# The first branch's triangular inverses on four 64x64 quarters of TensorE

## The chip, the cores and the metric

The kernel runs on one core of one Trainium2 chip. The metric is the device time of one execution in microseconds; the time before is the median of three runs. One more execution was profiled, and all rows of the trace below are from it. The engines are named as in the profile: PE is TensorE (matmuls), PEld its weight loads, DVE is VectorE, ACT is ScalarE, POOL is GpSimd.

## What is computed

The program is a small hybrid network on 256 tokens of 2048 channels: two attention layers (stages "L"), then one layer with two recurrent branches beside each other. The change touches only the first branch, a delta-rule recurrence with 16 heads of 64 channels that runs over 512 tokens (256 of the context, then 256 of the input) in both directions:

```python
def rwkv7_scan(r, decay, k, v, kk, b, s0, reverse, with_out):
    ...
    def step(s, inp):
        dec_t, k_t, v_t, kk_t, b_t = inp[:5]
        sa = jnp.einsum('bhvk,bhk->bhv', s, kk_t)
        s = (s * dec_t[:, :, None, :] - sa[..., None] * b_t[:, :, None, :]
             + v_t[..., None] * k_t[:, :, None, :])
```

The second branch is `gdn_chunked`, the gated delta rule with 8 heads of 128 channels, on the same tokens in both directions. Both are evaluated by chunks of 128 tokens. In a chunk the steps are coupled by a triangular matrix with ones on its diagonal, whose inverse is needed for each head, chunk and direction.

## The kernel before

**Stages.** The stages follow each other: L (two attention layers), P (projections of the recurrent layer), B (the two branches), C and M (merge and MLP). Stage B lies between about 1940 and 2875 us of the span.

**Threads of stage B.** A written order runs in stage B. Each engine has one instruction stream, and `Weave.run` makes it by taking one step (up to the next `yield`) of each stream in turn: `thread_a(0)`, `thread_b(0)`, `thread_a(1)`, `thread_b(1)`, then the tails and the bases. `thread_a(d)` is the first branch in direction d, for eight pairs of heads c = 0..7: `prep`, `scores`, `inverse`, `chain`. `thread_b(d)` is the second branch, for eight heads. So a step of an inverse of the first branch stands between steps of the other threads, on every engine, and engines take their streams in order. Direction 1 of a pair begins when direction 0 is 8 steps into its inverse (the word `middle`), so the two inverses of a pair don't overlap each other; the inverse of one direction lies beside the chain or the preparation of the other.

**An inverse.** For one (c, d) of the first branch there are eight 128x128 triangular matrices (2 heads x 4 chunks), in `NA`, 512 columns for a head. The inverse is built by doubling: `X` holds the inverses of the diagonal blocks of width w = 1, 2, 4, ... 32, and `XP` their transposes, for both 64-blocks of a matrix, which stand on the two halves of the partitions (0 to 63 and 64 to 127) with 64 columns for each matrix. Levels lv = 1 to 5 each do: `iq`, the product of NA's diagonal 64-blocks with X (16 matmuls of 64x64x64); DVE copies with a mask what lies beside the blocks into `Q` (L2555); `ix` and `it`, XP with Q and Q with XP (16 matmuls each); ACT copies the new halves of the blocks into X (its copies all stand at L1325), DVE those of XP (L2562), and POOL puts the identity back into Q (L3150). Level 0 is a masked copy (L2541, L2550). Level 6 joins the two 64-blocks: 8 matmuls from one partition half into the other, twice.

**Quarters of the array.** A 64x64x64 matmul takes its operands from one half of the partitions and writes one half of the partitions of a bank of PSUM, and so stands in one of four 64x64 quarters of the array: (rows, columns) = (low, low), (high, high), (low, high), (high, low). In levels 0 to 5 an operand's half is also its result's half, so only the first two quarters are used. The matmuls of level 6 all stand in a single crossed quarter. The second branch's inverse does the same with four matrices (`n == 4`), and it isn't changed. An fp32 matmul of the program is two MATMUL instructions in the profile, and each has its LDWEIGHTS.

**Banks.** Each direction of the first branch has a ring of two PSUM banks (`DR[d]`: banks 0 and 1, banks 2 and 3). The function `bank()` waits until the copy out of the bank's last use is done. `iq`, `ix` and `it` take a bank each, in turn.

## Time and profile before

| | us |
|---|---|
| median of 3 runs | 3850.47 |
| lowest, highest | 3849.56, 3851.57 |
| profiled execution, its own time | 3848.72 |
| its span on the core | 3846.6 |

The span is what the rows count in; 2.1 us of the execution lie around it, and the profiled execution is 1.75 us below the median of the three.

### The profile page before, as it was taken

Reading aid. Unit: us, or ns where it says so; the run is one execution under the profiler, and the core shown is the slowest. Engines: PE = TensorE matmul, PEld = TensorE weight load, DVE = VectorE, ACT = ScalarE, POOL = GpSimd, SP = SyncE. Lnnn points to the kernel's source line nnn. Section 1 sums busy time; section 2 is a strip of 40 time slices with the busy share of each in tenths; the row PEclk is TensorE's granted clock in tenths of the full one; section 3 lists DMA queues with packets and bytes.
Section 4 is the critical chain, followed back from the end, with each engine's and each line's share of the span. In section 5 each row is a group of like instructions: output and inputs, shape, how many; then the busy total and the mean of one; then the engine's idle time right before and its main releaser. Section 6 shows DMA issues by size and latency. Waiting matters only on the chain. (4 is left out here: it accounts for less than half of the span.)

```text
span 3846.6 us, 85962 instructions
## 1 busy us (share of the span) xinstructions
PE 3682.1 (96%) x37216; PEld 3409.0 (89%) x37216; DVE 2084.0 (54%) x3808; ACT 1504.8 (39%) x2641; POOL 1659.3 (43%) x1195
## 2 busy tenths in 40 slices
PE   7999999999998999999899999999988999999998
PEld 7999898999986888888688888888888999999998
DVE  5545425444336776677766666666547553435343
ACT  5344434444434432322233333333334453435353
POOL 5555556555544543333311111111115566666664
PEclk9999999999989999999999999999999999999999
DMA  6445454454445777778410000100007445455553
GB/s 238 169 180 181 187 196 156 167 185 176 175 154 175 259 261 266 250 258 293 154 32 20 15 24 28 28 20 15 3 2 263 176 176 187 177 186 184 179 186 131
DMA packets 116391, 587.20 MB, mean 153 GB/s; under 512 B 20912, under 2 KB 40496, under 8 KB 51376
## 3 DMA queue, kind: packets, MB, share of 16 engines
q1 hardware_dynamic: 116016, 581.71, 42.5%
q8 instruction: 295, 4.83, 0.5%
q14 instruction: 80, 0.66, 0.1%
HBM read 560.95 MB, written 20.71 MB: 151 GB/s over the span
## 5 line engine op out<-in xcount | busy, mean ns | idle before, releaser
L557 PE MATMUL bank<-act_L,part_L 128*128 128x256 f32 x7296 | 946.6, 288 | 12.4 <-DMA cst<-in_cst 4.6
L557 PEld LDWEIGHTS bank<-act_L,part_L 128*128 128x128 f32 x7296 | 901.0, 193 | 49.1 <-issue 30.6
L557 PE MATMUL bank<-act_P,part_P 128*128 128x512 f32 (+1 forms) x3488 | 716.1, 365 | 17.9 <-POOL part_P L3013 12.8
L3013 POOL TENSOR_TENSOR part_L<-wring,part_L 128x512 fp32r<-128x512 f32 x304 | 532.8, 1754 | 458.0 <-ACT part_L L1325 449.7
L3013 POOL TENSOR_TENSOR part_C<-wring,part_C 128x512 fp32r<-128x512 f32 x320 | 567.6, 1782 | 370.1 <-ACT part_C L1325 370.1
L557 PEld LDWEIGHTS bank<-act_P,part_P 128*128 128x128 f32 x3488 | 590.4, 188 | 136.9 <-DVE arena_P L2437 16.0
L557 PE MATMUL bank<-arena_B 64*64 64x64 f32 (+2 forms) x11200 | 544.4, 231 | 39.2 <-DVE arena_B L2550 21.0
L557 PEld LDWEIGHTS bank<-arena_B 64*64 64x64 f32 (+2 forms) x11200 | 481.3, 143 | 89.2 <-DVE arena_B L2550 23.4
L3013 POOL TENSOR_TENSOR part_P<-wring,part_P 128x512 fp32r<-128x512 f32 x184 | 306.1, 1669 | 428.1 <-ACT part_P L1325 428.1
L1325 ACT ACTIVATE part_C<-wring 128x1024 fp32r<-128x1024 f32 x320 | 338.4, 1058 | 355.8 <-PE bank L557 352.7
L557 PE MATMUL bank<-act_Y,part_C 128*128 128x258 f32 (+1 forms) x3840 | 463.7, 283 | 9.5 <-POOL part_C L3013 9.5
L557 PEld LDWEIGHTS bank<-act_Y,part_C 128*128 128x128 f32 x3840 | 462.9, 190 | 9.7 <-issue 9.7
L2040 DVE TENSOR_TENSOR part_L<-wring,part_L 128x512 fp32r<-128x512 f32 x304 | 239.5, 789 | 426.0 <-ACT part_L L1325 425.8
L557 PE MATMUL bank<-act_C,part_C 128*128 128x256 f32 x3840 | 468.5, 283 | 0.0
L557 PEld LDWEIGHTS bank<-act_C,part_C 128*128 128x128 f32 x3840 | 462.6, 192 | 0.0
L1325 ACT ACTIVATE part_L<-wring 128x1024 fp32r<-128x1024 f32 x304 | 320.6, 1056 | 293.5 <-PE bank L557 293.5
L2040 DVE TENSOR_TENSOR part_C<-wring,part_C 128x512 fp32r<-128x512 f32 x320 | 235.7, 736 | 297.9 <-ACT part_C L1325 297.8
L2101 DVE SCALAR_TENSOR_TENSOR arena_P<-arena_P,mods 128x512 f32<-128x512 f32 x240 | 272.8, 1137 | 8.1 <-DMA arena_P<-in_w 4.6
L2040 DVE TENSOR_TENSOR part_P<-wring,part_P 128x512 fp32r<-128x512 f32 x184 | 170.2, 925 | 190.9 <-ACT part_P L1325 190.8
L1325 ACT ACTIVATE part_P<-wring 128x1024 fp32r<-128x1024 f32 x184 | 191.2, 1053 | 153.0 <-PE bank L557 152.4
L3150 POOL COPY arena_B<-cst 128x256 f32<-128x256 f32 x80 | 32.5, 407 | 455.2 <-PE bank L557 455.2
L1325 ACT ACTIVATE arena_B<-bank 128x128 f32<-128x128 f32 (+4 forms) x296 | 111.2, 394 | 216.9 <-PE bank L557 119.3
(250 smaller groups left out, 3483.0 us busy)
## 6 DMA issues: line engine op xcount, KB each, us to landing
wring<-in_w SPq DMA_DIRECT2D x404, 1024.0 KB, 4.8
arena_P<-in_w SPq DMA_DIRECT2D x64, 1024.0 KB, 5.2
mring<-in_w SPq DMA_DIRECT2D x32, 1024.0 KB, 6.6
z_kept<-arena_P SPq DMA_DIRECT2D x34, 256.0 KB, 5.6
z_kept<-arena_P SPq DMA_DIRECT2D x58, 128.0 KB, 5.4
xT<-z_kept SPq DMA_DIRECT2D x26, 256.0 KB, 2.8
arena_C<-z_kept SPq DMA_DIRECT2D x32, 128.0 KB, 3.4
cst<-z_kept SPq DMA_DIRECT2D x24, 128.0 KB, 2.1
```

Source lines behind the costliest of these rows:

```text
L557: return e.matmul(out, lhsT, rhs, start=start, stop=stop)
L1325: return e.activation(out, a, ACT.Copy, scale=scale)
L2040: tt(wl[:, 0:4, :], wring[s % NS][:, 8 * j:8 * j + 4, :], wh[:, 0:4, :].bitcast(F32), sub).then_inc(*mark("dve_lo", "lov", stage, h))
L2101: z = ts(a, x, c, None, mult, None) if row == 0 else stt(a, x, c, a, mult, add)
L3013: e.tensor_tensor(wl[:, 4:8, :], wring[s % NS][:, 8 * j + 4:8 * j + 8, :], wh[:, 4:8, :].bitcast(F32), sub).then_inc(*mark("pool_lo", "lop ...
L3150: e.tensor_copy(region(Q[lv % 2], wd, d), same).then_inc(*mark(sem, "qf", tag, lv))
```

## The change

The first branch's inverses get functions of their own, `inverse_a`. Level 1 to 5 are computed with half of the eight matrices "straight" (as before) and half "crossed": of these, the block that stands on the low half is written to the high half and the other one to the low half. Which four of them cross changes with the level (`STRAIGHT`, `CROSSED`, `staying`, `moving`: pairs of matrices), so that operands always meet on one half. The matmuls are written in the order straight low, straight high, crossed low, crossed high, again and again. The straight ones write one bank of the ring, the crossed ones the other, so each of the two steps of a level takes both banks. Since a crossed result moves the whole transposed block, XP is copied whole for the four that move. The copies are now divided by bank: of `iq` two masked copies on DVE; of `it` two copies on ACT (from the straight bank) and two on DVE (from the crossed bank). `ix` and `it` are one step with one semaphore increment at its end. The transposes of level 0 are set by four masked copies instead of two. The masks (`lev2`) are twice as wide. Levels 0 and 6 have the matmuls that they had, and the number of steps (`yield`) of an inverse is the same. The threads, the loads and the other stages aren't touched.

```diff
@@ -545,6 +545,19 @@
 
         LATE_A, LATE_B, LATE_TA, LATE_TB, FIRST_B = 2, 3, 0, 0, 4
         CTXAT = (6, 8, 10, 12)
+
+
+        STRAIGHT = (slice(0, 4, 3), slice(0, 4, 2))
+        CROSSED = (slice(1, 3), slice(1, 4, 2))
+
+        def staying(lv):
+            return slice(0, 2) if lv < 5 else slice(0, 4, 2)
+
+        def moving(lv):
+            return slice(2, 4) if lv < 5 else slice(1, 4, 2)
+
+        def units(pairs):
+            return [2 * s + i for s in range(4)[pairs] for i in range(2)]
         GLA_LEAD, GLA_MORE = 3, 2
 
 
@@ -1026,6 +1039,80 @@
+            def inverse_a(tag, ring, NA, X, XP, Q):
...
+                def block(u, h):
+                    return NA[halves[h], 128 * u + 64 * h:128 * u + 64 * h + 64]
...
+                w.wait_ge(done("NA", tag))
+                b = bank()
+                for u in range(8):
+                    for h in range(2):
+                        t = mm(b[halves[h], cols(u)], block(u, h), C("id64")[halves[h], :], True, True)
+                t.then_inc(*mark("pe_inv", "iq", tag, 0))
+                yield
+                for lv in range(1, 6):
+                    straight, crossed = units(STRAIGHT[lv % 2]), units(CROSSED[lv % 2])
+                    stay, move = units(staying(lv)), units(moving(lv))
+                    w.wait_ge(done("X", tag, lv - 1))
+                    w.wait_ge(done("Xc", tag, lv - 1)) if lv > 1 else None
+                    b0, b1 = bank(), bank()
+                    for i in range(4):
+                        u, v = straight[i], crossed[i]
+                        for h in range(2):
+                            mm(b0[halves[h], cols(i)], block(u, h), X[halves[h], cols(u)], True, True)
+                        for h in range(2):
+                            t = mm(b1[halves[1 - h], cols(i)], block(v, h), X[halves[h], cols(v)], True, True)
+                    t.then_inc(*mark("pe_inv", "iq", tag, lv))
+                    yield
+                    w.wait_ge(done("Q", tag, lv))
+                    w.wait_ge(done("XT", tag, lv - 1))
+                    w.wait_ge(done("XTm", tag, lv - 1)) if lv > 1 else None
+                    b0, b1 = bank(), bank()
+                    q = Q[lv % 2]
+                    for i in range(4):
+                        u, v = straight[i], crossed[i]
+                        for h in halves:
+                            mm(b0[h, cols(i)], XP[h, cols(u)], q[h, cols(u)], True, True)
+                        for h in range(2):
+                            mm(b1[halves[1 - h], cols(i)], XP[halves[h], cols(v)], q[halves[h], cols(v)], True, True)
+                    for i in range(4):
+                        u, v = stay[i], move[i]
+                        for h in halves:
+                            mm(b0[h, cols(4 + i)], q[h, cols(u)], XP[h, cols(u)], True, True)
+                        for h in range(2):
+                            t = mm(b1[halves[1 - h], cols(4 + i)], q[halves[h], cols(v)], XP[halves[h], cols(v)], True, True)
+                    t.then_inc(*mark("pe_inv", "it", tag, lv))
...
+            def inverse_a(tag, ring, X, XP, XT):
...
+                for lv in range(1, 6):
+                    ring.take(), ring.take()
+                    yield
+                    (b, u), _ = ring.take(), ring.take()
+                    wd = 1 << lv
+                    w.wait_ge(done("it", tag, lv))
+                    cp(pairs(X, 4, wd, d)[:, STRAIGHT[lv % 2]], pairs(b[:, 0:256], 2, wd, d)).then_inc(*mark(V, "X", tag, lv))
+                    cp(pairs(XP, 4, wd, 1 - d)[:, staying(lv)], pairs(b[:, 256:512], 2, wd, 1 - d)).then_inc(*mark(V, "free", ring.name, u))
+                    counts.at[("XT", tag, lv)] = counts.last(V)
+                    yield
...
+            def inverse_a(tag, ring, NA, X, XP, XT, Q, before):
...
+                own(V)
+                for h in range(2):
+                    hs = slice(64 * h, 64 * h + 64)
+                    nv = NA[hs, :].rearrange("p (s u n two) -> p s u n two", s=4, u=2, two=2)[:, :, :, 32 * h:32 * h + 32, 1 - d]
+                    m0 = M("xt0", d * 32, 32)[hs, None, None, :].broadcast_to([64, 2, 2, 32])
+                    for out, which in ((hs, STRAIGHT[1]), (slice(64 - 64 * h, 128 - 64 * h), CROSSED[1])):
+                        xv = XP[out, :].rearrange("p (s u n two) -> p s u n two", s=4, u=2, two=2)[:, which, :, :, 1 - d]
+                        e.copy_predicated(xv, m0, nv[:, which]).then_inc(*mark(V))
+                counts.at[("XT", tag, 0)] = counts.last(V)
+                b, u = ring.take()
+                w.wait_ge(done("iq", tag, 0))
+                m0 = M("lev2", d * 6 * 64, 32)[:, None, :].broadcast_to([128, 8, 32])
+                e.copy_predicated(X.rearrange("p (u n two) -> p u n two", u=8, two=2)[:, :, :, d], m0,
+                                  b.rearrange("p (u n two) -> p u n two", u=8, two=2)[:, :, :, d]).then_inc(*mark(V, "free", ring.name, u))
+                counts.at[("X", tag, 0)] = counts.last(V)
+                yield
+                for lv in range(1, 6):
+                    wd = 1 << lv
+                    mk = M("lev2", (d * 6 + lv) * 64, 64).rearrange("p (m w) -> p m w", w=wd)[:, None, :, :].broadcast_to([128, 2, 64 // wd, wd])
+                    q = pairs(Q[lv % 2], 4, wd, d)
+                    use = [ring.take(), ring.take()]
+                    w.wait_ge(done("iq", tag, lv))
+                    w.wait_ge(done("qf", tag, lv - 2))
+                    for (b, u), which in zip(use, (STRAIGHT, CROSSED)):
+                        e.copy_predicated(q[:, which[lv % 2]], mk, pairs(b[:, 0:256], 2, wd, d)).then_inc(*mark(V, "free", ring.name, u))
+                    counts.at[("Q", tag, lv)] = counts.last(V)
+                    yield
+                    _, (b, u) = ring.take(), ring.take()
+                    w.wait_ge(done("it", tag, lv))
+                    e.tensor_copy(pairs(X, 4, wd, d)[:, CROSSED[lv % 2]], pairs(b[:, 0:256], 2, wd, d)).then_inc(*mark(V, "Xc", tag, lv))
+                    e.tensor_copy(XP.rearrange("p (s c) -> p s c", s=4)[:, moving(lv)], b[:, 256:512].rearrange("p (s c) -> p s c", s=2)).then_inc(
+                        *mark(V, "free", ring.name, u))
...
@@ -3150,6 +3316,7 @@
                     e.tensor_copy(region(Q[lv % 2], wd, d), same).then_inc(*mark(sem, "qf", tag, lv))
                     yield
                 w.wait_ge(done("XT", tag, 5))
+                w.wait_ge(done("XTm", tag, 5)) if n == 8 else None
                 e.tensor_copy(XT[0:64, :].rearrange("p (u s) -> p u s", u=n)[:, :, 0:64],
                               XP[0:64, :].rearrange("p (u s) -> p u s", u=n)).then_inc(*mark(sem, "XTp", tag))
                 yield
@@ -3456,6 +3623,10 @@
         for s, (kind, stage, h) in enumerate(TILES):
             if kind == "split":
                 tile_of[(stage, h)], tile_of[(stage, h + 1)] = (s, 0), (s, 1)
+
+        def pairs(buf, n, wd, side):
+
+            return buf.rearrange("p (s m two w) -> p s m two w", s=n, two=2, w=wd)[:, :, :, side, :]
 
...
```

**Order on PE.** This is the stream of PE in direction 1 of a pair, from the first branch's `iq` of one level to its next `ix`; bank2 and bank3 belong to the first branch, bank5 to the second branch's inverse. Before:

```order
L557 MATMUL bank3<-arena_B 64x64 [waits s_act_rwkv]
L557 MATMUL bank3<-arena_B 64x64 x15
L557 MATMUL bank5<-arena_B 64x64 [waits s_dve_gdn,s_act_gdn]
L557 MATMUL bank5<-arena_B 64x64 x7
L557 MATMUL bank1<-wring2,arena_B 128x64 [waits s_act_rwkv]
L557 MATMUL bank1<-wring2,arena_B 128x64
L557 MATMUL bank4<-arena_B 128x128 [waits s_dve_gdn]
L557 MATMUL bank2<-arena_B 64x64 [waits s_dve_rwkv]
L557 MATMUL bank2<-arena_B 64x64 x15
L557 MATMUL bank3<-arena_B 64x64 x16
```

The same kind of place in the change, an `iq` with the rows around it:

```order
L570 MATMUL bank1<-wring2,arena_B 128x64 [waits s_act_rwkv]
L570 MATMUL bank1<-wring2,arena_B 128x64
L570 MATMUL bank4<-arena_B 128x128 [waits s_dve_gdn]
L570 MATMUL bank3<-arena_B 64x64 [waits s_act_rwkv,s_dve_rwkv]
L570 MATMUL bank3<-arena_B 64x64
L570 MATMUL bank2<-arena_B 64x64 x2
L570 MATMUL bank3<-arena_B 64x64 x2
...
L570 MATMUL bank5<-arena_B 64x64 [waits s_dve_gdn]
L570 MATMUL bank5<-arena_B 64x64 x7
```

Sixteen matmuls into one bank have become sixteen that change bank after every two, and the wait ahead of the `iq` (which stood on ACT alone) now names both ACT and DVE.

**Order on DVE.** The copies of one level in direction 1, before: L2555 is the masked copy into Q, L2562 the copy into XP, the rest belongs to other threads.

```order
L2555 COPY_PREDICATED arena_B<-msk,bank3 128x32x8 [waits s_pool_rwkv,s_pe_inv]
L2555 COPY_PREDICATED wring1<-msk,bank5 128x32x4 [waits s_pe_inv]
L2026 TENSOR_SCALAR wring0<-cst,par 128x256 [waits s_dve_gdn,s_dma_bq]
L2797 SCALAR_TENSOR_TENSOR wring0<-cst,par,wring0 128x255 [waits s_dve_gdn]
L2799 SCALAR_TENSOR_TENSOR wring0<-cst,par,wring0 128x255 [waits s_dve_gdn]
L2771 SCALAR_TENSOR_TENSOR arena_B<-bank4,par,arena_B 128x128 [waits s_pe_chain]
L2562 COPY arena_B<-bank3 128x32x8 [waits s_pe_inv]
```

In the change, L2721 is the masked copy, L2726 the copy into X and L2727 that into XP; L2670 and L2677 are those of the second branch:

```order
L2721 COPY_PREDICATED arena_B<-msk,bank3 128x2x16x4 [waits s_pe_inv]
L2721 COPY_PREDICATED arena_B<-msk,bank2 128x32x4
L2670 COPY_PREDICATED wring1<-msk,bank5 128x64x2 [waits s_pe_inv]
L2726 COPY arena_B<-bank2 128x32x4 [waits s_pe_inv]
L2727 COPY arena_B<-bank2 128x256
L2677 COPY arena_B<-bank5 128x64x2 [waits s_pe_inv]
L2945 SCALAR_TENSOR_TENSOR arena_B<-arena_B,par,bank4 128x128 [waits s_dve_gdn,s_pe_chain]
```

One copy of each kind has become two of half the width, with one that moves whole blocks (128x256).

## Rows read from the trace of the kernel before

**Rows 1.** The page's first part: busy us (share of the span) x instructions.

```profile
PE 3682.1 (96%) x37216; PEld 3409.0 (89%) x37216; DVE 2084.0 (54%) x3808; ACT 1504.8 (39%) x2641; POOL 1659.3 (43%) x1195
```

**Rows 2.** Busy time by stretch; the second is one pair of heads.

```profile
core 0: us, PE busy (x) PEld busy (x) DVE busy (x) ACT busy (x) POOL busy (x), PEclk, DMA share, GB/s
1940.00:2875.00 935.00, 883.23 (x16507) 794.77 (x16502) 577.52 (x1430) 323.82 (x908) 147.09 (x258) 0.99 0.07 19
...
2162.67:2280.99 118.32, 111.67 (x2106) 100.48 (x2106) 76.10 (x188) 41.81 (x117) 19.28 (x33) 1.00 0.09 23
```

**Rows 3.** Whom PE waited for, 1940 to 2875: us, times, longest.

```profile
PE bank L557 <- DVE arena_B L2550: 21.0, 16, 1.6
PE bank L557 <- POOL smalls L3018: 11.6, 12, 1.2
```

**Rows 4.** Page part 5: the 64x64 matmuls.

```profile
L557 PE MATMUL bank<-arena_B 64*64 64x64 f32 (+2 forms) x11200 | 544.4, 231 | 39.2 <-DVE arena_B L2550 21.0
```

**Rows 5.** PE by stretch: level 6 alone, then ix and it.

```profile
core 0: us, PE busy (x), PEclk, DMA share, GB/s
2143.62:2144.39 0.77, 0.77 (x14) 1.00 0.00 0
...
2138.53:2140.44 1.91, 1.91 (x65) 1.00 0.00 0
```

**Rows 6.** PE in order of time, 2196.5 to 2197.0: start, us.

```profile
2196.61 0.27 PE L557 MATMUL bank<-wring,arena_B 64*64 64x64 f32 x2
2196.66 0.22 PE L557 MATMUL bank<-arena_B 64*64 64x64 f32 x1
2196.72 0.22 PE L557 MATMUL bank<-wring,arena_B 64*64 64x64 f32 x1
2196.72 0.22 PE L557 MATMUL bank<-arena_B 64*64 64x64 f32 x1
2196.72 0.27 PE L557 MATMUL bank<-wring,arena_B 64*64 64x64 f32 x2
2196.78 0.22 PE L557 MATMUL bank<-arena_B 64*64 64x64 f32 x1
```

**Rows 7.** Groups of DVE, 1940 to 2875: busy us, mean ns | idle before.

```profile
L2555 DVE COPY_PREDICATED arena_B<-msk,bank 128x256 f32<-128x256 uint8 x78 | 38.2, 490 | 64.0 <-PE bank L557 64.0
L2562 DVE COPY arena_B<-bank 128x256 f32<-128x256 f32 x79 | 33.6, 425 | 99.0 <-PE bank L557 99.0
L2555 DVE COPY_PREDICATED wring<-msk,bank 128x128 f32<-128x128 uint8 x80 | 25.7, 321 | 12.4 <-PE bank L557 11.2
L2562 DVE COPY arena_B<-bank 128x128 f32<-128x128 f32 x80 | 23.2, 289 | 29.5 <-PE bank L557 29.2
L2541 DVE COPY_PREDICATED arena_B<-msk,arena_B 64x256 f32<-64x256 uint8 x30 | 22.3, 743 | 1.0
...
L2541 DVE COPY_PREDICATED arena_B<-msk,arena_B 64x128 f32<-64x128 uint8 x32 | 14.1, 442 | 1.1
```

**Rows 8.** Groups of ACT in the same stretch.

```profile
L1325 ACT ACTIVATE arena_B<-bank 128x256 f32<-128x256 f32 x95 | 36.4, 383 | 69.9 <-PE bank L557 69.1
L1325 ACT ACTIVATE arena_B<-bank 128x128 f32<-128x128 f32 x111 | 30.9, 278 | 134.9 <-DVE arena_B L2562 85.9 <-PE bank L557 48.8
```

**Rows 9.** In order of time, level 1's ix and it to level 2's iq.

```profile
2164.52 2.40 PE L557 MATMUL bank<-arena_B 128*128 128x128 f32 x66
...
2166.96 0.43 DVE L2562 COPY arena_B<-bank 128x256 f32<-128x256 f32 x1 [1.67 <-PE bank L557]
...
2167.23 1.85 PE L557 MATMUL bank<-arena_B 128*128 128x64 f32 x37
```

**Rows 10.** By stretch: levels 1 to 5 of direction 0; levels 4 and 5 of direction 1.

```profile
2162.67:2195.86 33.19, 33.19 (x671) 29.66 (x671) 14.33 (x41) 10.40 (x30) 4.06 (x8) 1.00 0.01 2
2245.77:2253.55 7.78, 7.56 (x157) 6.11 (x156) 6.47 (x13) 3.77 (x11) 0.70 (x2) 1.00 0.27 70
2253.55:2261.95 8.40, 8.40 (x176) 8.02 (x177) 6.41 (x19) 3.37 (x10) 3.06 (x5) 1.00 0.07 20
```

**Rows 11.** By stretch: before and in a fall of the granted clock.

```profile
2278.00:2281.60 3.60, 2.02 (x46) 1.79 (x43) 2.85 (x6) 0.28 (x1) 0.00 (x0) 1.00 0.00 0
2281.60:2285.00 3.40, 3.40 (x38) 3.06 (x34) 1.08 (x2) 0.62 (x2) 0.00 (x0) 0.50 0.02 5
```

More of the change, by code:

```diff
@@ L40 @@
     CSTN += _w
[L41 to L42 removed]
+MSK = {"strict": (0, 256), "incl": (256, 256), "lev2": (512, 768), "xt0": (1280, 64), "gla": (1344, 1024)}
+MSKN = 2368
 def constants():
@@ L1144, in thread_a @@
                     yield from scores(c, d)
-                    yield from weave.after(8, ("middle", c) if d == 0 else None, inverse((c, d), DR[d], g.NA, g.X, g.XP, g.Q, 8))
+                    yield from weave.after(8, ("middle", c) if d == 0 else None, inverse_a((c, d), DR[d], g.NA, g.X, g.XP, g.Q))
                     yield from chain(c, d)
@@ L1723, in inverse @@
                 yield
+            def inverse_a(tag, ring, X, XP, XT):
+                d = tag[-1]
+                e_ = slice(64 - 64 * d, 128 - 64 * d)
+                V = "act_rwkv"
+                ring.take()
+                yield
+                for lv in range(1, 6):
+                    ring.take(), ring.take()
+                    yield
+                    (b, u), _ = ring.take(), ring.take()
[4 more added lines that the diff above has]
+                    counts.at[("XT", tag, lv)] = counts.last(V)
+                    yield
+                b, u = ring.take()
+                w.wait_ge(done("iq", tag, 6))
+                cp(X[e_, :], b[e_, :]).then_inc(*mark(V, "free", ring.name, u))
+                counts.at[("Q", tag, 6)] = counts.last(V)
+                w.wait_ge(done("XT", tag, 5))
+                w.wait_ge(done("XTm", tag, 5))
+                cp(XT[64:128, :].rearrange("p (u s) -> p u s", u=8)[:, :, 64:128], XP[64:128, :].rearrange("p (u s) -> p u s", u=8)).then_inc(
+                    *mark(V, "XTa", tag))
+                yield
+                ring.take()
+                yield
             def prep(c, d):
@@ L1816, in thread_a @@
                     yield from scores(c, d)
-                    yield from weave.after(8, ("middle", c) if d == 0 else None, inverse((c, d), DR[d], g.X, g.XP, g.XT, 8, "act_rwkv"))
+                    yield from weave.after(8, ("middle", c) if d == 0 else None, inverse_a((c, d), DR[d], g.X, g.XP, g.XT))
                     yield from chain(c, d)
```

57 lines of the change are left out of this document (48 added, 9 removed).

## The prediction

> **What bounds the kernel now.** I read the shares first: PE is busy for 96% of the span and no other engine for more than 54% [rows 1]. The change touches stage B alone, so the question is whether PE bounds that stage too. In its 935 us PE is busy for 883 us, DVE for 578 and ACT for 324 [rows 2]. One pair of heads takes 118.3 us, of which PE works 111.7. The view of waits says what ends PE's few pauses there: 21.0 us stand behind the masked copy of level 0 (16 waits, one for each inverse), 11.6 us behind POOL's roots [rows 3]. So PE sets the time of stage B, and a microsecond taken from its stream counts, as long as the copies between two steps stay covered by the other threads' matmuls. The 64x64 matmuls are a large part of that stream: 544 us of busy time [rows 4].
>
> **What a 64x64 matmul costs.** The mean of 231 ns in [rows 4] is a latency; what counts is how often one can start. When level 6 uses one quarter alone, 14 instructions start in 0.77 us, 55 ns apart. When ix and it use two quarters, 65 start in 1.91 us, 29.4 ns apart [rows 5]. Each quarter thus takes one instruction in 55 to 59 ns, whether its neighbour works or not. The question of the whole case is whether a third and a fourth quarter do the same. The trace has a place with three: at 2196.61 the last matmuls of level 6 (arena_B alone, a crossed quarter) are still running when the second branch's (wring,arena_B, the two straight quarters) begin [rows 6]. From the arena_B start at 2196.66 to the one at 2196.78, its quarter keeps 58 to 60 ns, and three wring instructions of the two straight quarters start in between (a row of x2 that begins at 2196.72 and lasts 0.27 has its second start about 0.05 after its first): three quarters at their full pace. The crossed quarter shares its rows with one straight quarter and its columns with the other, and neither costs anything. Nothing that I see says that the fourth is different, and I take 58.6/4 = 14.65 ns.
>
> The Trainium skill, in "TensorE: Matmul & The Clock Gate", section "Wait — 56ns, not 53.3ns?", speaks against this change: starts of matmuls never come closer than about 25 ns on average, however small they are. By that step 1 of the sum would be 7680 x 4.4 ns = 34 us in place of 113. In [rows 6] three instructions start at 2196.72 and two more by 2196.78, so the trace disagrees as far as it goes, but it shows this for a moment and not for a run of 64.
>
> **The sum.**
> 1. *Matmuls.* Levels 1 to 5 have 48 matmuls, 96 instructions, each; there are 16 inverses, so 80 levels and 7680 instructions. At 29.4 - 14.65 = 14.75 ns each this takes away 113 us. Their number doesn't change, nor do levels 0 and 6.
> 2. *Level 0.* The two masked copies of 743 ns become four of half the width, which take 442 ns in the second branch's inverse [rows 7]. That is 0.28 us more, and it lies ahead of the very copy for which PE waits [rows 3], so all of it counts: 16 x 0.28 = 4.5 us lost.
> 3. *Q.* One masked copy of 490 ns becomes two of 321 ns [rows 7]: 0.15 us later. Between iq and ix stand the other threads' steps, and their length isn't changed; at level 2 of direction 0, the tightest place that I found, this still fits. Nothing, with up to 0.1 us a level (8 us) at the low end of the gain.
> 4. *X and XP.* Before, ACT could copy X while `it` was still running, and XP's copy was needed one step later. Now `iq` needs both banks and so all four copies: 2 x 278 ns on ACT [rows 8], 289 + 425 = 714 ns on DVE [rows 7], all begun after the last matmul. The cover is the work of the other threads between `it` and the next `iq`. The shortest that I found is behind level 1 of direction 0: PE's 66 instructions end at 2164.52 + 2.40 = 2166.92, DVE's copy begins 0.04 us later, and the next iq starts at about 2167.93, since the row of 37 ends at 2169.08 and an iq lasts 1.15 us [rows 9]. So 1.01 us of cover stand against 0.04 + 0.71 and about 0.1 for the signal to PE. It fits, if DVE and ACT are free. If every one of the 80 levels missed by 0.3 us, that would be 24 us.
> 5. *DVE where it is full.* The new copies cost DVE 0.15 + 714 - 425 ns = 0.44 us a level and 35 us in all, beside 578 busy us [rows 2]. In direction 0 there is room: 14.3 of 33.2 us. In levels 4 and 5 of direction 1, where DVE also prepares the next pair, it is busy for 12.9 of 16.2 us [rows 10]. There PE would need only 16.2 - 2.8 = 13.4 us, and DVE has 12.9 + 0.9 = 13.8 us with some waits of its own left. I take 1.4 us of the 2.8 as lost for each of the 8 pairs: 11 us.
> 6. *Other waits that lose their cover.* POOL's roots cost PE 12 waits of about 1 us now [rows 3]; with 14 us less of PE's work in each pair, about one more will show, and the end of level 5 in direction 0 runs into the DVE-heavy stretch behind it. An estimate from these rows: 1.3 us a pair, 10 us.
>
> 113 - 4.5 - 11 - 10 = 87 us. From the profiled execution's 3848.7 that gives 3761.7, and with the 1.75 us by which the median of the runs lies above it, 3763.5. I say **3764 us**, 2.2% less than the median of 3850.5. The masks' larger load at the start and SBUF's 96 more words are no term: neither stands ahead of PE's first matmuls in the written order.
>
> **The rivals.**
> - *DVE takes the bound.* The copies aren't hidden: DVE or ACT, which take their streams in order, come late to them because another thread's operation stands ahead. For it: [rows 10], and that both banks must now be empty. Against it: DVE's mean load after the change, 578 + 40 of about 850 us, is 73%. If each level misses by 0.5 us beyond the sum (40 us), the time is about 3804; the Trainium skill, "TensorEngine Tiling (Array Packing)", section "PSUM Bottleneck", warns of just this. I see 3795 to 3835, chance 0.11.
> - *The quarters don't run four abreast.* A floor on starts, or a path for operands that crossed and straight quarters share when both are busy for long. For it: no row has four. Against it: [rows 6]. If nothing is gained the starts stay at 29.4 ns and the time is 3850.5 + 4.5 = 3855; if three abreast are the limit, 58.6/3 = 19.5 ns, step 1 gives 76 us and the sum 50, 3800. I put the case at 3806 to 3856, chance 0.05. The floor of the Trainium skill's page named above would give 34 - 4.5 us, since with so little taken from PE the copies stay covered: 3821.
> - *Slower, by the two-bank wait.* One mechanism: the four copies between `it` and `iq`. Before, half of this latency was hidden behind `it` itself. If the wait for them (and the mask copies) grows by more than 1.3 us in each of the 80 levels (104 us and more), the change loses. That needs the copies to end 2.3 us behind `it` even where the cover is only 1.0 us, and their own durations with the signals give 0.85; the decisive point is a mean wait of PE of 1.3 us ahead of `iq`. For it speaks only that in [rows 10] the two late levels of direction 1 might do so. 3858 to 3880, chance 0.03.
> - A term of either sign is the clock. After a stretch in which PE works 2.02 of 3.60 us the granted clock is 0.50 for 3.4 us (1.2 in place of 2.4 GHz), in which PE is busy throughout [rows 11]. Such a fall costs up to 1.7 us. The weak stretches lie in the preparation, which the change leaves alone, but new waits may make more of them: five falls more are 8 us. It widens the range and decides nothing.
>
> **How the numbers follow.** The forecast has 0.81: it holds from 3737 (terms 2 to 6 all nothing and the full 113 us) to 3795 (items 3 to 6 twice as large). With the first rival's nearer half the range is 3738 to 3806. A measurement of this kernel can tell 0.2%, 7.7 us. Faster by more than that are the forecast, the first rival and most of the second: 0.94. Within 0.2% is the rest of the second and the edge between the cases: 0.03. Slower: 0.03.
>
> **What the changed profile would show.** Two windows tell step 1: in a joined ix and it, 64 instructions should start in about 0.95 us, where 65 took 1.91; in an iq 32 in about 0.47. A pair of heads should take 107 to 108 us for 118.3. The waits of PE should show the masked copy of level 0 with about 25 us for 21, and new lines for ACT's L1412 and DVE's copies of the first branch, together 10 to 25 us, mostly in levels 4 and 5 of direction 1. DVE's busy time should rise by about 40 us (35 and level 0's 4.5), ACT's by 2 x 278 - 383 ns = 0.17 us a level, 14 us. If the instructions start 14 to 15 ns apart and the time is still above 3800, steps 4 to 6 are wrong; if they start 25 ns apart, step 1 is.

## The result and the profile after

The changed kernel takes **3790.83 us** (median of 4 runs, 3786.40 to 3791.33), against 3850.84 for the kernel before beside it: 60.0 us or 1.6% less, ratio 0.984 with a 95% interval of 0.983 to 0.985. The forecast was 3764, range 3738 to 3806. The sign and the range hold, but 27 of the forecast's 87 us didn't come. The profiled execution took 3791.04 us, its span 3789.0.

The page's first part and the windows of stage B answer to [rows 1, 2]. The columns are those of [rows 2]; the second row is one pair of heads, the third levels 1 to 5 of direction 0 in another pair:

```profile
PE 3601.8 (95%) x37216; PEld 3321.8 (88%) x37216; DVE 2102.6 (55%) x4000; ACT 1508.5 (40%) x2721; POOL 1660.3 (44%) x1195
```

```profile
1940.00:2820.00 880.00, 805.36 (x16480) 709.53 (x16469) 599.31 (x1620) 330.07 (x991) 148.71 (x258) 0.96 0.07 20
2154.24:2266.59 112.35, 103.06 (x2104) 90.94 (x2104) 78.89 (x213) 42.46 (x127) 19.41 (x33) 0.95 0.08 24
2266.59:2293.54 26.95, 26.48 (x670) 22.82 (x671) 15.54 (x53) 10.69 (x35) 4.05 (x8) 1.00 0.01 3
```

A pair took 118.3 us (four of the seven that can be measured from start to start) and now takes 110.0 to 113.0. The five levels of direction 0 took 33.2 us [rows 10] and now take 27.0 in this pair: 6.2 less, of the 5 x 1.4 = 7.0 that the matmuls alone give. But read the column PEclk: over the stage it fell from 0.99 [rows 2] to 0.96, and in this pair from 1.00 to 0.95. And PE's idle time in the stage grew, from 935 - 883 = 52 us [rows 2] to 880 - 805 = 75.

PE alone, an iq and a joined ix and it (they answer to [rows 5]):

```profile
2340.89:2341.37 0.48, 0.48 (x32) 1.00 0.08 11
2344.52:2345.46 0.94, 0.94 (x64) 1.00 0.00 0
```

64 instructions in 0.94 us are 14.7 ns each; 65 took 1.91 before. PE's waits answer to [rows 3]:

```profile
PE bank L570 <- DVE arena_B L2709: 24.8, 15, 1.9
PE bank L570 <- POOL smalls L3184: 10.4, 12, 0.9
PE bank L570 <- ACT wring L1412: 9.0, 10, 1.1
PE bank L570 <- DVE arena_B L2141: 5.3, 7, 0.8
PE bank L570 <- ACT wring L1409: 4.9, 8, 0.6
PE bank L570 <- ACT arena_B L1412: 4.1, 5, 3.2
```

L2709 is level 0's masked copy. Copies of X and XP (L2726 with 1.1 us, which isn't shown, and a part of ACT's arena_B L1412) stand low: together less than 6 us.

**Where it went.** From the traces' starts I took, for each pair and direction, the time from one level's first iq matmul to the next level's, and summed it over the eight pairs; behind the slash stands how much of it lay at a granted clock of 0.50 (of 1.00, that is 1.2 in place of 2.4 GHz). "filled" is the run e4_fill, "more" is e9_more_fill, both below.

| us, eight pairs | before | after | filled | more |
|---|---|---|---|---|
| dir. 0, level 0 to 1 | 29.6/4 | 31.5/4 | 31.6/4 | 19.0/4 |
| 1 to 2 | 45.4/10 | 35.2/10 | 31.6/0 | 38.5/0 |
| 2 to 3 | 53.5/0 | 42.5/0 | 42.5/0 | 42.5/0 |
| 3 to 4 | 56.2/0 | 45.6/0 | 45.6/0 | 45.6/0 |
| 4 to 5 | 59.6/0 | 50.5/0 | 50.5/0 | 50.5/0 |
| 5 to 6 | 46.9/0 | 40.8/0 | 40.8/0 | 40.8/0 |
| level 6 | 36.6/4 | 33.4/0 | 34.9/5 | 33.4/0 |
| dir. 1, level 0 to 1 | 37.3/0 | 39.5/0 | 39.5/0 | 39.5/0 |
| 1 to 2 | 68.6/0 | **68.5/20** | 61.7/0 | 61.7/0 |
| 2 to 3 | 62.0/0 | 54.6/0 | 54.5/0 | 54.5/0 |
| 3 to 4 | 54.3/0 | 43.1/0 | 43.1/0 | 43.2/0 |
| 4 to 5 | 59.8/0 | **60.2/0** | 60.3/0 | 60.1/0 |
| 5 to 6 | 64.6/0 | **70.6/38** | 60.7/7 | 60.7/7 |
| level 6 | 26.8/0 | 26.1/0 | 23.3/0 | 23.3/0 |
| dir. 0's end to dir. 1's first iq | 142.4/13 | 142.3/10 | 145.7/29 | 142.9/6 |

A level's matmuls gained 8 x 1.4 = 11 us. Direction 0 shows most of it. Direction 1 lost it in the three bold rows, and two of them now have 58 us at the lower clock, where before there was none.

Level 4 of direction 1, and level 5 behind it, in one pair (they answer to the last two of [rows 10]); the third row is the fall itself:

```profile
2340.89:2348.93 8.04, 6.50 (x157) 4.70 (x157) 7.60 (x19) 4.03 (x12) 1.44 (x3) 1.00 0.19 68
2348.93:2359.02 10.09, 10.09 (x177) 9.56 (x177) 5.81 (x17) 3.35 (x10) 2.36 (x5) 0.66 0.06 15
2350.20:2357.00 6.80, 6.80 (x111) 6.46 (x111) 3.80 (x15) 1.84 (x6) 1.50 (x3) 0.50 0.01 4
```

In level 4 PE now works 6.50 of 8.04 us (7.56 of 7.78 before) and DVE 7.60. In level 5 PE is busy throughout, and for 6.80 us of it at half clock. How much that costs can be read from the eight pairs: without a fall this level takes 7.85 us (five pairs of e9_more_fill), with one fall of 3.4 us 8.5, with two 10.1 (four pairs of the changed kernel). So a fall costs 0.7 us here and two 2.2, less than half of their length each, since at full clock PE would wait a little more. What holds level 4 is seen on ACT and DVE in order of time:

```profile
2343.86 0.49 DVE L2141 TENSOR_SCALAR wring<-cst,par 128x512 f32<-128x512 f32 x1
2344.38 0.75 DVE L2963 SCALAR_TENSOR_TENSOR wring<-cst,par,wring 128x510 f32<-128x510 f32 x1
2345.17 0.75 DVE L2965 SCALAR_TENSOR_TENSOR wring<-cst,par,wring 128x510 f32<-128x510 f32 x1
```

```profile
2345.95 0.63 ACT L1409 ACTIVATE wring<-wring 128x512 f32<-128x512 f32 x1 [2.50 <-DVE wring L2965]
2346.49 0.40 ACT L1409 ACTIVATE wring<-cst 128x256 f32<-128x256 f32 x1
2346.79 0.40 ACT L1409 ACTIVATE wring<-wring 128x256 f32<-128x256 f32 x1
2347.10 1.24 ACT L1409 ACTIVATE arena_B<-bank,par 128x512 f32<-128x512 f32 x2
2348.24 0.60 ACT L1412 ACTIVATE arena_B<-bank 128x128 f32<-128x128 f32 x3
```

The second branch's convolution for the next head (a multiplication and two multiply-adds in a chain on DVE, each for q, k and v; the rows show L2141, L2963 and L2965) ends at 2345.92. ACT has waited 2.50 us for it, does four more operations of other steps, and only at 2348.24 copies X and XP. `it` had ended 2.6 us earlier. The first two of the three copies in that row are those of X and XP, and they end at 2348.67 (the third is the second branch's); PE passes its waits for them and for DVE's copies one after the other, and iq starts at 2348.93. (The view of waits books such pauses under DVE L2141, 5.3 us in 7 waits: an operation of the preparation that ends at about the same time, for which iq doesn't wait.)

### The profile page after: what moved, and what is told of

It is laid out like the page before. It is cut to its first block and busy times, and to the rows that moved or that the text cites. A ratio compares the mean times of both kernels' runs of the same rounds, so it can differ in the third digit from the quotient of the medians.

```text
span 3789.0 us, 86299 instructions
## 1 busy us (share of the span) xinstructions
PE 3601.8 (95%) x37216; PEld 3321.8 (88%) x37216; DVE 2102.6 (55%) x4000; ACT 1508.5 (40%) x2721; POOL 1660.3 (44%) x1195
## 5 line engine op out<-in xcount | busy, mean ns | idle before, releaser
L570 PE MATMUL bank<-act_L,part_L 128*128 128x256 f32 x7296 | 946.2, 288 | 12.7 <-POOL act_L L3220 7.1
L570 PE MATMUL bank<-act_P,part_P 128*128 128x512 f32 (+1 forms) x3488 | 715.9, 365 | 18.0 <-POOL part_P L3179 12.7
L570 PE MATMUL bank<-arena_B 64*64 64x64 f32 (+2 forms) x11200 | 447.0, 237 | 51.0 <-DVE arena_B L2709 24.8
L1412 ACT ACTIVATE part_C<-wring 128x1024 fp32r<-128x1024 f32 x320 | 337.8, 1057 | 357.7 <-PE bank L570 355.3
L570 PEld LDWEIGHTS bank<-arena_B 64*64 64x64 f32 (+2 forms) x11200 | 381.8, 147 | 103.5 <-DVE arena_B L2709 27.2
L1412 ACT ACTIVATE part_L<-wring 128x1024 fp32r<-128x1024 f32 x304 | 320.2, 1054 | 293.7 <-PE bank L570 293.7
L1412 ACT ACTIVATE part_P<-wring 128x1024 fp32r<-128x1024 f32 x184 | 190.9, 1051 | 153.1 <-PE bank L570 152.4
L570 PE MATMUL bank<-wring,arena_B 64*64 64x64 f32 (+3 forms) x2208 | 193.1, 254 | 7.4 <-DVE arena_B L2817 3.1
```

The source lines that it names most:

```text
L570: return e.matmul(out, lhsT, rhs, start=start, stop=stop)
L1412: return e.activation(out, a, ACT.Copy, scale=scale)
```

## The experiments

**My theory** after this: step 1 is right in full; the missing 27 us are (a) falls of the clock behind the new weak stretches, (b) a larger loss in direction 1 than forecast, where DVE and ACT hold the steps. **Rivals**: the gain came from something other than the four quarters; the two-bank wait costs something in all levels; the lower clock is only a by-product. Twelve kernels ran. Each difference below is that of the medians of a kernel and of the kernel before on the same chip; the changed kernel stands at -60.0.

| run | median us | before | difference | ratio, 95% interval |
|---|---|---|---|---|
| e1_two_abreast | 3819.14 | 3849.57 | -30.4 | 0.992 (0.990 to 0.994) |
| e8_runs_of_16 | 3843.72 | 3851.39 | -7.7 | 0.998 (0.997 to 0.999) |
| e3_dir0_only | 3807.04 | 3849.57 | -42.5 | 0.989 (0.988 to 0.991) |
| e2_x0_first | 3794.92 | 3849.57 | -54.7 | 0.985 (0.983 to 0.987) |
| e4_fill | 3772.71 | 3849.57 | -76.9 | 0.980 (0.978 to 0.981) |
| e7_before_fill | 3852.67 | 3851.39 | +1.3 | 1.001 (1.000 to 1.002) |
| e5_fill_x0 | 3771.49 | 3851.39 | -79.9 | 0.979 (0.978 to 0.981) |
| e9_more_fill | 3762.29 | 3852.75 | -90.5 | 0.977 (0.975 to 0.978) |
| e6_two_taps | 3786.47 | 3851.39 | -64.9 | 0.983 (0.982 to 0.985) |
| e10_fill_taps | 3753.67 | 3852.75 | -99.1 | 0.974 (0.973 to 0.976) |
| e12_act_copies | 3762.06 | 3851.48 | -89.4 | 0.977 (0.976 to 0.978) |
| e11_copy_twice | 3792.62 | 3852.75 | -60.1 | 0.985 (0.983 to 0.986) |

### Is it the four quarters? (e1, e8)

```diff
                     for i in range(4):
-                        u, v = straight[i], crossed[i]
+                        u = straight[i]
                         for h in range(2):
                             mm(b0[halves[h], cols(i)], block(u, h), X[halves[h], cols(u)], True, True)
+                    for i in range(4):
+                        v = crossed[i]
                         for h in range(2):
                             t = mm(b1[halves[1 - h], cols(i)], block(v, h), X[halves[h], cols(v)], True, True)
```

The loops of ix and it are split in the same way; in e8 both straight loops of ix and it stand ahead of both crossed ones.

> The changed kernel with one thing undone: in every step of levels 1 to 5 all straight matmuls stand ahead of all crossed ones, so that at most two quarters work side by side. Copies, banks and waits are those of the changed kernel. If the gain is all four quarters at once, starts fall back to about 29 ns and 7680 instructions give back 7680 x 14.5 ns = 111 us at most; with the copies covered again as before, the time is that of the kernel before plus level 0's 4.5 us and little more: 3853 to 3870. If a part of the gain came from elsewhere (two banks, another split of the copies), it stays below 3840. If the new copies cost much by themselves (the two-bank wait), it goes above 3880.

> As the run e1_two_abreast, but in the step of ix and it all 16 straight matmuls stand ahead of all 16 crossed ones (iq keeps 8 and 8). In e1_two_abreast, where they changed over every 8 matmuls, the starts came 21.3 ns apart over the 64 instructions, not 29, so instructions of the crossed quarters ran while straight ones were still queued. If each quarter has a short queue of its own, longer runs fill it: starts 24 to 26 ns apart, 5 to 10 us on top of 3819, so 3823 to 3832. If the pace doesn't depend on the length of a run, the time is 3819 again.

Measured: half of the gain stayed in e1. By its expectation a part of the gain would then come from elsewhere, and the first rival would live. But the trace shows that the edit didn't do what I had said of it: the starts didn't fall back to 29 ns. The window of one joined ix and it of e1 and of e8 (PE alone; 12 and 14 of the instructions belong to the neighbouring steps, the 64 are spread over all of it):

```profile
2339.74:2341.09 1.35, 1.35 (x76) 1.00 0.21 47
```

```profile
2345.34:2347.02 1.68, 1.68 (x78) 1.00 0.40 109
```

So 64 took 1.35 us (21 ns each) in runs of 8 matmuls, and 1.68 us (26 ns) in runs of 16; an iq with runs of 8 starts every 24.4 ns in both. Instructions of the other kind start while those ahead in program order still wait for their quarter. The end of that window of e8 shows it:

```profile
2346.68 0.27 PE L570 MATMUL bank<-cst,arena_B 64*64 64x64 f32 x2
2346.73 0.28 PE L570 MATMUL bank<-arena_B 64*64 64x64 f32 x3
...
2346.86 0.22 PE L570 MATMUL bank<-arena_B 64*64 64x64 f32 x1
```

The rows with cst,arena_B are the second branch's next step, in straight quarters, and stand behind all of ix and it (arena_B) in the program; their first starts 0.17 us ahead of the last crossed one of `it`. Per level e1 saves 96 x 29.4 - 32 x 24.4 - 64 x 21.3 = 0.68 us of PE's time, e8 0.36, the change 1.40: 54, 29 and 112 us over 80 levels. (From iq to iq, levels 2 and 3 of direction 0 are 0.69, 0.34 and 1.35 us shorter than before.) The kernels gained 30, 8 and 60. Copies and banks are the same in all three, so the gain follows the pace of the matmuls, with a little over half of it coming through (less in e8). Nothing is left for the rival: with less of the pace, less of the gain remained, and nothing beyond it. For e8 I had the starts right (24 to 26 ns) and the time 12 us too low.

The two traces show something else. From the first iq of the stage to the last inverse, e1 and e8 have 80 and 76 us at half clock (e8 in the fastest of its ten executions, 3836.88 us), nearly as much as the changed kernel (83), where the kernel before has 31. So the falls don't come in proportion to the work taken from PE: e8 took away only a quarter of it. What the three share, and the kernel before lacks, are the copies, the banks and the waits; which of these brings the falls isn't shown.

### Which direction? (e3)

> The change in direction 0 alone; direction 1 has the inverse of before. By the segments of the two traces, direction 0 gained about 53 us in levels 1 to 5 and direction 1 only some 11 net (nothing in its levels 1, 4 and 5). If that reading is right, most of the gain stays: 3798 to 3806. If both directions are worth the same, half the gain of 60 us stays: 3820. If direction 1's DVE load of the changed form costs more than its matmuls save, it is below 3791.

-42.5 with direction 0 alone, so direction 1 adds 17.5 of the 60.0. That is 1 us above the expected stretch; the segments of direction 0 are to 0.1 us those of the changed kernel in levels 2 to 5.

### The clock (e4, e7)

```diff
+                    if lv == 1:
+                        b0 = bank()
+                        mm(b0[halves[0], :], block(0, 0), NA[halves[0], 0:512], True, True)
                     w.wait_ge(done("X", tag, lv - 1))
...
                 w.wait_ge(done("tw"))
+                if d == 0:
+                    mm(b[0:64, 0:256], C("id64")[0:64, :], D.tw[0:64, 0:256], True, True)
...
+                if fill:
+                    mm(b[0:64, :], C("id64")[0:64, :], C("scan")[0:64, :], True, True)
                 w.wait_ge(done("sq", tag))
```

The second place is the preparation's first projection, the third the sums, where `fill` is set for q alone.

> The changed kernel with matmuls added whose results are overwritten and never read, at places where PE waits: one of 64x64 by 512 columns (about 0.85 us at full clock) in each of the 16 waits for the masked copy of level 0, one ahead of the sums of the second branch's q in each of 8 heads (0.85 us), and one of 256 columns ahead of the first projection of direction 0's preparation (0.43 us). They take no work off any engine: DVE's and ACT's streams are untouched. If the lower granted clock behind weak stretches takes a part of the gain (some 17 falls, 75 us at 1.2 GHz in stage B, of them 58 us in levels 1 and 5 of direction 1), fewer falls come and the time falls to 3765 to 3782, with level 5 of direction 1 back to 7 us each. If the falls are only a by-product of waits that end when they end, the time is the same or, since the added matmuls take PE's time where the wait is shorter than they, up to 5 us longer: 3790 to 3797.

> The kernel before with the added matmuls of the run e4_fill, a control. The kernel before has 5 falls, about 24 us at 1.2 GHz, in stage B, none in levels 1 and 5 of direction 1. If the added matmuls help only by the falls that the change brought, there is little to win here: 3843 to 3853. If they help in some other way (shorter waits, another order), they do it here too and the time falls by about the same 18 us, to 3832.

Adding work made the kernel 16.9 us faster. In the table above the column "filled" differs from "after" where "after" had the lower clock (and in places that the falls moved to): 68.5 to 61.7 and 70.6 to 60.7 in direction 1, 35.2 to 31.6 in direction 0. The levels that ran at 1.00 stay within 0.1 us, but for level 6 of direction 1, behind the falls (26.1 to 23.3). The same two stretches as above, in e4_fill:

```profile
2334.66:2342.66 8.00, 7.40 (x161) 4.88 (x161) 7.54 (x19) 4.04 (x12) 1.35 (x3) 1.00 0.19 68
2342.66:2350.51 7.85, 7.27 (x177) 6.70 (x177) 6.57 (x19) 3.16 (x10) 2.43 (x5) 1.00 0.07 20
```

Level 4 lasts as long (8.00), only that PE is busy for 7.40 of it and not 6.50; and level 5 behind it goes from 10.09 us to 7.85 at a clock of 1.00. In the control, the same matmuls in the kernel before change nothing in the sum (+1.3, within the noise), though they cut its wait for level 0's masked copy from 21.0 [rows 3] to 7.4 us in the view of waits:

```profile
PE bank L557 <- DVE arena_B L2556: 7.4, 15, 0.5
```

A wait that is filled is no wait that is gone. But the sum hides two parts. Level 4 of direction 1 has hardly a wait in the kernel before, and there the eight added matmuls cost 6.9 us (59.8 to 66.7), while levels 0 and 1 of direction 0 became 4.3 us shorter and the 10 us at half clock there went. So the control doesn't show that the fillers have no effect there; it shows that they don't win without the new falls. With e4, where the gain stands in the levels that had fallen, this says that the changed kernel lost time to falls that it brought itself.

### Level 0 (e2, e5)

e2 moves the masked copy of X on DVE ahead of the four of XP; e5 does this in direction 0 alone, on top of e4.

> The changed kernel with one move: at level 0 the masked copy of X stands ahead of the four masked copies of XP on DVE, so that the wait of PE ahead of the iq of level 1 (24.8 us in 15 waits, 1.6 us each) ends up to 1.8 us earlier. If this wait sets the time, the next operations (the first is needed by PE one step later) don't: up to 16 x 1.5 = 24 us less, 3767. DVE's work is the same, and in direction 1 two waits for DVE follow right behind iq, so I expect the wait to be passed on in part: 3773 to 3785. If DVE alone sets this place, nothing comes back: 3788 to 3792.

> The kernel of the run e4_fill with one more edit: in direction 0 alone, the masked copy of X at level 0 stands ahead of the four of XP. In the run e2_x0_first this took 12.9 us from the way between the iq of levels 0 and 1 of direction 0 (31.5 to 18.6 us) and gave 2.7 us back one level later; in direction 1 it was all given back. If the two savings (waits at level 0, falls of the clock) are separate, 3772.7 - 10 = 3762, between 3759 and 3766. If the added matmuls and the earlier copy fight for the same wait (the fill lasts 0.85 us and the wait would have been over sooner), the gain is less than 4 us: 3769 to 3774.

e2 is 5 us slower than the change by its median, and my expectation (3773 to 3785) was missed. The profiled execution is the fast one of its four (3779.88); the figures by segment are from it. PE got its X earlier (31.5 to 18.6 and 39.5 to 25.5 us in the two level-0 rows), but DVE's work was the same, and PE then waited for the next thing that DVE makes, an operand of the second branch:

```profile
PE bank L570 <- DVE arena_B L2915: 15.5, 9, 2.0
```

Level 1 to 2 of direction 1 grew from 68.5 to 83.9. One run took 3779.88 us at a mean clock of 0.978, the other three 3794.6 to 3796.1 at 0.973: 0.005 of 3790 us is 38 us at half clock and so up to 19 us, and 15 were seen. At a mean clock near the changed kernel's (0.976) the earlier copy was worth up to 11 us; in three runs of four the clock took it back. e5 repeats this in direction 0: 12.7 us gained at level 0, 7 lost one level later, and the falls went to the end of direction 0 (level 6 at 38.7 us, 15 at half clock; 40 us behind it). 3.0 us were left, no more than the medians of the kernel before differ from chip to chip (3849.57 to 3852.75).

### Filling the other waits (e9)

```diff
             def spread(ring, tag, sm, n, heads):
                 b, u = ring.take()
                 w.wait_ge(free(ring, u))
+                if tag[0] in ("y", "o"):
+                    mm(b[0:64, :], C("id64")[0:64, :], C("scan")[0:64, :], True, True)
```

> The kernel of the run e5_fill_x0 with a further added matmul (64x64 by 512 columns, overwritten, never read) ahead of each of the 16 spreads of the output norms, where PE waits about 1 us for POOL's root. In e5_fill_x0 the falls had left levels 1 and 5 of direction 1, but 55 us at 1.2 GHz stood between level 6 of direction 0 and the first iq of direction 1, where these two spreads lie (30 to 39 us more than in the changed kernel), and they ate the 10 us of the earlier copy. If what PE does not do in a wait decides on the falls there too, most of them go and up to 20 us with them: 3753 to 3764. If the falls only move on to the next stretch with waits, the time stays: 3766 to 3773.

-90.5, 10.6 better than e5, and the largest gain of a kernel that computes everything: 3762.29 us. Stage B and one pair:

```profile
1940.00:2790.00 850.00, 808.70 (x16552) 688.46 (x16550) 598.65 (x1619) 328.51 (x989) 148.40 (x257) 0.99 0.07 20
2145.67:2253.30 107.63, 103.22 (x2118) 87.64 (x2120) 78.90 (x213) 42.33 (x127) 19.39 (x33) 1.00 0.09 26
```

PEclk is back at 0.99, and a pair takes 107.6 us, what the prediction had said of the changed kernel.

### Level 4 of direction 1: DVE's stream (e6, e10, e12)

e6 and e10 leave out one tap of the convolution for k and v, so their output is another; e12 gives DVE's two copies of X and XP to ACT in direction 1.

```diff
-                    stt(wv[:, :, 1:256], zv[:, :, 0:255], P("conv", n, 1), wv[:, :, 1:256], mult, add).then_inc(*mark(V))
-                    own(V)
+                    if key == "q":
+                        stt(wv[:, :, 1:256], zv[:, :, 0:255], P("conv", n, 1), wv[:, :, 1:256], mult, add).then_inc(*mark(V))
+                        own(V)
```

> The changed kernel without the middle tap of the second branch's convolution for k and v (the output differs by that): two multiply-adds of DVE of 0.75 us fewer for each of 8 heads, nearly all in level 4 of direction 1, where DVE runs without a gap for 8 us. PE and ACT do what they did. If DVE's stream is what holds level 4 of direction 1 at 8.0 us, it falls to 6.5 to 7 (8 to 12 us in all), and the stretch of 1.2 GHz behind it gets shorter (up to 10 us more): 3768 to 3782. If the level is bound by the second branch's sums and roots or by the projection's banks, the time moves by less than 3 us.

> The kernel of the run e9_more_fill, again without the middle tap of the convolution for k and v (the output differs by that). In e6_two_taps this took 10.6 us from level 4 of direction 1 (60.2 to 49.6 us) and the falls behind it went, but 41 us more of falls at other places gave most of it back, and the whole came to 4 us. If the two are separate (DVE's stream holds level 4, the clock takes its part elsewhere), then with the waits filled the full 10 us show: e9_more_fill less 8 to 12 us. If again less than 5 us come out, filling does not decouple them.

> The kernel of the run e9_more_fill, with DVE relieved in direction 1: all four copies of X and XP behind it are made by ACT, which takes 0.70 us a level off DVE's stream (40 levels) and puts two more short copies on ACT, 0.16 us apart. In e9_more_fill, with the falls of the clock gone, direction 1 is still short of its matmul gain by some 26 us (levels 1, 2, 4 and 5). If DVE's stream by its length is what holds these levels, each gives some tenths back: 8 to 16 us, 3746 to 3755. If in level 4 it is the order of the streams (ACT's copies of X stand behind two of its operations that wait for DVE's convolutions, and those convolutions are a chain) only a little comes back: 3756 to 3762. If ACT's longer queue delays iq, it is slower than 3764.

e6 made the stretch from level 4 to 5 shorter by 10.6 us (60.2 to 49.6), and took the falls out of level 5 (60.7, none). In one pair:

```profile
2338.95:2345.43 6.48, 6.16 (x158) 4.78 (x157) 5.36 (x13) 4.04 (x12) 0.69 (x2) 1.00 0.27 84
```

So the convolution on DVE holds this level. Yet the kernel gained only 4.9 us, less than expected: the falls came at other places (levels 1 of both directions 24 and 27 us at half clock), and stage B's clock is the lowest of all profiles:

```profile
1940.00:2818.00 878.00, 811.33 (x16546) 715.85 (x16546) 592.52 (x1613) 330.30 (x993) 151.33 (x259) 0.94 0.07 20
```

With the waits filled (e10) the same edit is worth 8.6 us; level 4 then gives 4.6 (60.1 to 55.5), where e6 gave 10.6, probably because a filler costs time once the wait is shorter than it (e7). e12 shows which part of DVE's stream matters. The copies that it takes from DVE (whose busy time falls from 2103 to 2085 us) stand behind the convolution, and in level 4 of the pair above, counted from its iq, the convolution ends at 5.02 us in e12 as in e9: nothing ahead of it moved. ACT's two further copies stand ahead of the next iq, which starts at 8.38 us for 8.04. By level, e12 gave 3.7 us in level 2 (54.5 to 50.8) and took 2.5 and 2.3 in levels 4 and 5; the whole is the same (-89.4 for -90.5). So DVE's copies hold a part of level 2, and level 4 is held by what stands ahead of the convolution's end on DVE and behind it on ACT. What holds levels 1 and 5 of direction 1 below their gain isn't shown.

### The two-bank wait (e11)

```diff
+                    if d == 0:
+                        e.tensor_copy(XP.rearrange("p (s c) -> p s c", s=4)[:, moving(lv)], b[:, 256:512].rearrange("p (s c) -> p s c", s=2)).then_inc(*mark(V))
+                        own(V)
```

> The changed kernel with the copy of XP on DVE made twice in direction 0 (the second after the first), which delays the two-bank wait ahead of each iq by about 0.5 us in levels 2 to 6 of 8 inverses. In the changed kernel the copies end 0.33, 2.2, 1.4 and 2.0 us ahead of the iq of levels 2 to 5. If the copies are covered as the prediction's step 4 says, only level 2 (short by 0.2) and what DVE delays for others shows: direction 0 longer by 1 to 6 us in all, levels 3 to 5 by nothing. If the copies between it and iq had no cover, 40 x 0.5 = 20 us would be added: 3811.

No change in the whole (-60.1). By segment: levels 2 to 5 of direction 0 take 42.8, 45.5, 50.5 and 40.8 us for 42.5, 45.6, 50.5 and 40.8. The cover is real there. Level 1, where it is only 0.3 us, can't be read: it took 41.7 us for 35.2, with 24 us at half clock for 10. Level 5 of direction 1 made up for it (64.5 for 70.6, 24 us for 38), so that the sum came out the same is partly luck.

## Why the prediction was right, and by how much it was off

1. **Matmuls, -113.** Right. 32 x 14.9 and 64 x 14.7 ns are 1.42 us a level; with the 2.82 of before this is 1.40 and 112 us. The Trainium skill ("TensorE: Matmul & The Clock Gate", "Wait — 56ns, not 53.3ns?") says that starts are never less than about 25 ns apart; the row of 64 in 0.94 us disagrees, and the measurement decides.
2. **Level 0, +4.5.** Right: 1.9 + 2.2 = 4.1.
3. **Q, nothing.** Right, and as tight as said: in levels 1 and 2 of direction 0 the masked copies end 0.2 us before PE comes to ix.
4. **X and XP, nothing.** Right in direction 0: the copies are there 0.3, 2.2, 1.4 and 2.0 us ahead of the iq of levels 2 to 5, and e11 shows that half a microsecond more changes nothing. In direction 1 the copies on DVE end 1.2 us or more ahead of the next iq in seven of the eight pairs, but behind level 4 ACT is late by its queue. The waits for the copies came to about 10 us with those booked under L2141, the low end of the 10 to 25 that I had said.
5. **DVE where it is full, +11.** The place was right and the size too small. Levels 4 and 5 of direction 1 in "filled" (60.3 and 60.7, the latter with 7 us at half clock) gained -0.5 and 3.9 of 11.2 each: 19 lost. I had balanced DVE's busy time (13.8 us) against PE's, as if any order would do. Level 4 is held by a chain: convolution on DVE, then ACT's queue, then X (e6, e12). Levels 1 and 2 of direction 1 lost 4 each besides, where I had seen nothing. And it wasn't for more work on DVE: its busy time rose by 22 us in the stage (578 to 599), not by 40, and ACT's by 6, not 14, since two short copies in a row overlap (the row of two masked copies in a step lasts 0.49 us, like the one of before). With half of the load forecast, the loss was more than twice the forecast.
6. **Other waits, +10.** About right in size: direction 0 lost 9 in its five levels, 5 of them in level 5. But POOL's roots didn't grow (10.4 for 11.6).
7. **The clock, "it widens the range and decides nothing".** With term 5 this is the step that failed. I had allowed for five falls more, 8 us, as width and not in the sum. Direction 1 got 58 us at half clock that it hadn't had, and against "filled" they cost 6.8 us in level 1 and 9.9 in level 5, together 17.

Between the two profiled executions the gain is 57.7, so 29 of the 87 us are missing: 17 by the clock, 27 lost in direction 1's levels for the 11 forecast, 1 less in direction 0, 1 in the matmuls, and 4 gained in level 6, which I hadn't counted: 17 + 16 - 1 + 1 - 4 = 29. The clock and term 5 thus missed by about the same, and that the time still lies in the range is owed to the range's width on the slow side, not to these terms. Two numbers of that range don't follow from the text: terms 3 to 6 twice as large give 3785 and not 3795, and "three abreast" at 3800 lies outside the stretch given to its own case.

**Of the rivals**, "DVE takes the bound" (3795 to 3835) is shown at two levels of ten (levels 4 and 2 of direction 1) and isn't true of the kernel; the floor on starts is refuted by the row of 0.94 us, and "slower by the two-bank wait" by the time itself and, for levels 2 to 5 of direction 0, by e11. The pair of heads at 107 to 108 us was missed (110.0 to 113.0). e9, with its waits filled and one level-0 wait shortened, has 107.6 in most pairs; that it meets the number is partly chance, since its levels 1, 2, 4 and 5 of direction 1 still lose what term 5 lacked, and the shortened wait gives some back. What stays open: why a fall comes at one place and not at another. The runs show that falls leave a place whose waits are filled and turn up at another with waits (e2, e5, e6), not what decides it. Nor do they simply follow PE's idle time: from the first iq to the last inverse it fell from 51 to 32 us between the kernel before and e7, and the time at half clock rose from 31 to 38.

## What to carry to other kernels

When a change takes work from TensorE and leaves the other engines' chains alone, its waits become longer (52 to 75 us of idle time here), and a granted clock that was 1.00 may fall behind them; price that as a term of its own, with a look at which stretches will have waits back to back. It needn't be small when the gain is: e8 had nearly all the falls for a quarter of the work. Where a wait can't be removed, a matmul that nobody reads, put ahead of the wait into a bank that is free, can win time back (16.9 us here, 27 with those of e9). Where there is no wait it costs its own length (6.9 us in e7). In a stretch where an engine is nearly full, follow the one chain that ends last through the queues instead of comparing busy times.

## What the runs showed of the hardware

- Four 64x64 quarters take fp32 instructions 14.7 ns apart, which is 58.8 ns for each, as with two (2 x 29.4). No cost of sharing rows or columns was seen.
- With the two kinds of quarters in turns of 8 and 16 matmuls the starts are 21 and 26 ns apart, not 29: those of the other kind don't wait for their turn in the program: in e8 instructions of the next step start 0.17 us ahead of the last of the step before.
- The same kernel can have two mean granted clocks: e2 had 0.978 once and 0.973 three times, 15 us apart.
- A stretch at half clock costs less than half of its length where PE also waits: one of 3.4 us cost 0.7 us in level 5 of direction 1, two cost 2.2.
